# A hybrid decoder layer on one core: logits of b and a with stationary weights, and a last output finished by token halves

## The reference

```python
h = rms_norm(x, norm1_g[l])
proj = h @ w_in[l]                      # two groups of 16 columns are b_logit and a_logit
beta = jax.nn.sigmoid(b_logit)
g = -jnp.exp(a_log) * jax.nn.softplus(a_logit + dt_bias)
...
x = x + jnp.square(jax.nn.relu(h @ w_ff_up[l])) @ w_ff_down[l]
return rms_norm(x, final_norm_g)        # x * rsqrt(mean(x*x) + eps) * gain, per token and channel
```

## Time and profile before

| | |
|---|---|
| median of three runs | 1945.68 us (1942.75, 1945.68, 1945.89) |
| the profiled execution, its own time | 1942.99 us |
| its span, from first to last instruction | 1941.2 us |
| mean granted TensorE clock | 0.989 |
| busy: PE, DVE, ACT, POOL | 97%, 57%, 46%, 6% |
| traffic | 316.36 MB, 163 GB/s |

### The profile page before, as it was taken

How to read it: one execution, slowest core, us unless ns; L and a number is a source line. 1 busy time by engine, 2 the same in 40 slices (tenths; PEclk the granted TensorE clock), 3 DMA queues, 4 the chain that set the end, 5 groups by cost and what they waited for, 6 DMA issues and landing times.

```text
span 1941.2 us, 29129 instructions
## 1 busy us (share of the span) xinstructions
PE 1885.3 (97%) x10816; PEld 1554.7 (80%) x10816; DVE 1099.7 (57%) x1438; ACT 885.4 (46%) x1382; POOL 120.6 (6%) x86
## 2 busy tenths in 40 slices
PE   7998998998998999999999999999999999999997
PEld 6887877877877888888888888888888888888886
DVE  5366676676676665666555555555544455555544
ACT  5344345354354345555444445444433344444442
POOL 0005014014014000000000000000000000000000
PEclk9899999999999999999999999999999999999999
DMA  7353333333333354444456666555555555555553
GB/s 256 126 163 119 110 131 109 110 130 109 115 124 115 114 167 152 141 152 141 161 195 201 201 199 208 183 189 177 191 192 192 192 190 189 185 186 192 195 191 124
DMA packets 87953, 316.36 MB, mean 163 GB/s; under 512 B 9648, under 2 KB 10160, under 8 KB 87728
## 3 DMA queue, kind: packets, MB, share of 16 engines
q1 hardware_dynamic: 86992, 312.64, 48.9%
q0 software_dynamic: 576, 2.10, 0.4%
q10 hardware_dynamic: 288, 0.18, 0.0%
HBM read 312.79 MB, written 2.10 MB: 162 GB/s over the span
## 4 chain that ended last, share of the span: by engine, by line
PE 53%; issue 38%; DVE 3%; POOL 3%; ACT 1%; DMA 0%; DVEq 0%; ACTq 0%; POOLq 0%; SPq 0%
PE acc L287 15%; PE acc L289 14%; PE acc L288 14%; PE J L384 4%; PE J L432 1%; PE J L316 1%; POOL rg L1418 1%; PE J L423 1%; ACT w_hi L653 1%; PE J L440 1%; DVE cT L1051 1%; DVE qn L1051 1%; PE J L475 1%; PE J L304 0%; POOL mats L1440 0%
## 5 line engine op out<-in xcount | busy, mean ns | idle before, releaser
L996 DVE TENSOR_TENSOR w_lo<-raw,w_hi 128x1024 fp32r<-128x1024 f32 x584 | 725.3, 1244 | 638.0 <-ACT w_hi L653 636.6
L653 ACT ACTIVATE w_hi<-raw 128x1024 fp32r<-128x1024 f32 x584 | 618.7, 1061 | 681.7 <-PE acc L289 679.0
L287 PE MATMUL acc<-w_hi,hT_hi 128*128 128x512 f32 x1440 | 582.1, 404 | 8.9 <-issue 4.4
L289 PE MATMUL acc<-w_hi,hT_lo 128*128 128x512 f32 x1440 | 564.7, 392 | 0.0
L288 PE MATMUL acc<-w_lo,hT_hi 128*128 128x512 f32 x1440 | 564.5, 392 | 0.0
L287 PEld LDWEIGHTS acc<-w_hi,hT_hi 128*128 128x128 f32 x1440 | 272.4, 189 | 71.8 <-issue 8.4
L289 PEld LDWEIGHTS acc<-w_hi,hT_lo 128*128 128x128 f32 x1440 | 272.1, 189 | 58.7
L288 PEld LDWEIGHTS acc<-w_lo,hT_hi 128*128 128x128 f32 x1440 | 272.6, 189 | 52.5 <-issue 1.0
L287 PE MATMUL acc<-w_hi,act_hi 128*128 128x512 f32 x512 | 199.3, 389 | 0.0
L289 PE MATMUL acc<-w_hi,act_lo 128*128 128x512 f32 x512 | 199.2, 389 | 0.0
L288 PE MATMUL acc<-w_lo,act_hi 128*128 128x512 f32 x512 | 199.2, 389 | 0.0
(11 more groups left out here) (210 smaller groups left out, 1522.4 us busy)
## 6 DMA issues: line engine op xcount, KB each, us to landing
raw<-weights SPq DMA_DIRECT2D x584, 512.0 KB, 3.3
xres<-x SPq DMA_DIRECT2D x4, 512.0 KB, 7.5
xres<-x POOLq DMA_DIRECT2D x4, 512.0 KB, 5.6
y<-nat SPq DMA_DIRECT2D x4, 512.0 KB, 2.7
fgain_sb<-fgain SPq DMA_DIRECT2D x1, 1024.0 KB, 5.2
masks_sb<-masks SPq DMA_DIRECT2D x1, 640.0 KB, 11.0
zs<-w_ba SPq DMA_DIRECT2D x1, 256.0 KB, 9.9
dist_sb<-dist SPq DMA_DIRECT2D x1, 192.0 KB, 3.4
```

The costliest lines, as they stand in the source:

```text
L287: mm(o, aT_hi[:, kt, tok], w_hi[:, c % RING, w], start=(c == 0 and k == 0), stop=False)
L289: last = mm(o, aT_lo[:, kt, tok], w_hi[:, c % RING, w], start=False, stop=(c == nch - 1 and k == CK - 1))
L653: A(w_hi[:, slot], raw[:, slot], ACT.Copy).then_inc(hi_ready, 1)
L996: tt(w_lo[:, slot], raw[:, slot], w_hi[:, slot].bitcast(F32), ALU.subtract).then_inc(lo_ready, 1)
```

## The change

**Logits.** The weights become the stationary operand (128 x 32) and the activations move, 256 tokens at once: 16 row tiles x 3 matmuls, 48 in all, into `J[0:32, 1, 0:256]`, channels on partitions. DVE copies that to `baT` (in `kn`, not yet in use) at h = 20, PE transposes it in two operations at h = 21 into `J[:, 0]`, where the logits stood before, and DVE's and ACT's decay chain is at h = 22.

**Last output.** Its last four chunks, all four in the ring, are multiplied first for tokens 0 to 127, then for tokens 128 to 255 (`by_halves`). Each half has its own add, square, sums, power, multiplications and four transfers of 256 KB. The channel weight of the first three quarters is multiplied in by POOL while the down projection runs, that of the last quarter by DVE; what is left at the end is a multiplication by the row factor, three of them on DVE and one on ACT for each half. The squares' unused results go to other places. The declarations of semaphores are left out below.

```diff
@@ -174,6 +174,7 @@
         ba = vb[:].rearrange("p t n -> p (t n)")
+        baT = kn[0:32, 0, 0:T]
         kdup = rawg[:, 0]
@@ -255,20 +258,38 @@
             stream(OUT_FF * CPO // RING, N_CHUNKS // RING)
-            for i in range(4):
-                sp.wait_ge(y_ready, i + 1)
-                sp.dma_start(out[:, :, i * NB:(i + 1) * NB], nat[:, :, i * NB:(i + 1) * NB]).then_inc(y_out, 16)
-            sp.wait_ge(y_out, 16 * 4)
+            for t in range(NT):
+                for n, (i, s_done, v) in enumerate(((0, y_dve, 3 * t + 1), (2, y_act, t + 1), (1, y_dve, 3 * t + 2), (3, y_dve, 3 * t + 3))):
+                    sp.wait_ge(s_done, v)
+                    sp.dma_start(out[:, t, i * NB:(i + 1) * NB], nat[:, t, i * NB:(i + 1) * NB]).then_inc(y_out, 16)
+            sp.wait_ge(y_out, 16 * 4 * NT)
...
-            def output(c0, par, aT_hi, aT_lo, free, jobs=None, nch=CPO, h0=0, before=None):
-
-
-                for c in range(nch):
+            def product(par, t, aT_hi, aT_lo, c, k, first, last):
+                kt = c * CK + k
+                w, tok, o = slice(k * NB, (k + 1) * NB), slice(t * P, (t + 1) * P), acc[:, par, t]
+                mm(o, aT_hi[:, kt, tok], w_hi[:, c % RING, w], start=first, stop=False)
+                mm(o, aT_hi[:, kt, tok], w_lo[:, c % RING, w], start=False, stop=False)
+                return mm(o, aT_lo[:, kt, tok], w_hi[:, c % RING, w], start=False, stop=last)
+
+            def by_halves(c0, par, aT_hi, aT_lo, nch):
+
+                for t in range(NT):
+                    for c in range(nch - RING, nch):
+                        if t == 0:
+                            pe.wait_ge(lo_ready, c0 + (c + 1))
+                        for k in range(CK):
+                            ins = product(par, t, aT_hi, aT_lo, c, k, False, c == nch - 1 and k == CK - 1)
+                    ins.then_inc(half_used, 1)
+
+            def output(c0, par, aT_hi, aT_lo, free, jobs=None, nch=CPO, h0=0, before=None, end=None):
+
+
+                for c in range(nch if end is None else end):
                     if before:
@@ -279,15 +300,8 @@
                     for k in range(CK):
-                        kt = c * CK + k
-                        w = slice(k * NB, (k + 1) * NB)
                         for t in range(NT):
-                            tok = slice(t * P, (t + 1) * P)
-                            o = acc[:, par, t]
-                            mm(o, aT_hi[:, kt, tok], w_hi[:, c % RING, w], start=(c == 0 and k == 0), stop=False)
-                            mm(o, aT_hi[:, kt, tok], w_lo[:, c % RING, w], start=False, stop=False)
-                            last = mm(o, aT_lo[:, kt, tok], w_hi[:, c % RING, w], start=False,
-                                      stop=(c == nch - 1 and k == CK - 1))
+                            last = product(par, t, aT_hi, aT_lo, c, k, c == 0 and k == 0, c == nch - 1 and k == CK - 1)
                         if k == CK - 1:
@@ -497,15 +511,19 @@
                     pe.wait_ge(wba_ready, 2)
+                    for kt in range(KT):
+                        w = slice(kt * 32, (kt + 1) * 32)
+                        o = J[0:32, 1, 0:T]
+                        mm(o, wba_hi[:, w], hT_hi[:, kt, :], start=(kt == 0), stop=False)
+                        mm(o, wba_lo[:, w], hT_hi[:, kt, :], start=False, stop=False)
+                        ins = mm(o, wba_hi[:, w], hT_lo[:, kt, :], start=False, stop=(kt == KT - 1))
+                    ins.then_inc(ba_done, 1)
+                if h == 21:
+
+                    pe.wait_ge(baT_ready, 1)
                     for t in range(NT):
-                        tok = slice(t * P, (t + 1) * P)
-                        for kt in range(KT):
-                            w = slice(kt * 32, (kt + 1) * 32)
-                            o = J[:, 0, t * 32:(t + 1) * 32]
-                            mm(o, hT_hi[:, kt, tok], wba_hi[:, w], start=(kt == 0), stop=False)
-                            mm(o, hT_hi[:, kt, tok], wba_lo[:, w], start=False, stop=False)
-                            ins = mm(o, hT_lo[:, kt, tok], wba_hi[:, w], start=False, stop=(kt == KT - 1))
-                    ins.then_inc(ba_done, 1)
+                        ins = tr(J[:, 0, t * 32:(t + 1) * 32], baT[:, t * P:(t + 1) * P], ident[0:32, 0:32])
+                    ins.then_inc(ba_T, 1)
                 if h == 32:
@@ -634,7 +652,9 @@
                            [(relu_sq, r0 + 7 + d)] if d < 2 else [(x_added, x0 + d - 1)],
-                           last_T if d == 0 else None, nch=2 * CPO)
+                           last_T if d == 0 else None, nch=2 * CPO,
+                           end=2 * CPO - RING if hf == 1 and d == FF_DOWN - 1 else None)
+            by_halves(N_CHUNKS - 2 * CPO, 1 - (FF_DOWN - 1) % 2, act_hi, act_lo, 2 * CPO)
@@ -681,7 +701,7 @@
                 for t in range(NT):
-                    ins = A(dst[:, t, w], xres[:, t, w], ACT.Square, accum_out=part[:, t, i:i + 1])
+                    ins = A(dst[:, t], xres[:, t, w], ACT.Square, accum_out=part[:, t, i:i + 1])
                 ins.then_inc(ssq_x, 1)
@@ -838,7 +858,7 @@
                     A(wba_hi[:], w_ba_sb, ACT.Copy).then_inc(wba_ready, 1)
-                if h == 20:
+                if h == 22:
@@ -928,17 +948,17 @@
-            def add_squares(n, first):
+            def add_squares(n, first, dst):
...
                         act.wait_ge(x_added, first + n)
-                        squares(n - 1, nat)
+                        squares(n - 1, dst)
                 return job
...
             for i in range(4):
-                output((OUT_WO + i) * 2, turn_pair(2, i - 1, add_squares(i, 0)) if i else turn_last(1), lambda: None)
+                output((OUT_WO + i) * 2, turn_pair(2, i - 1, add_squares(i, 0, nat[:, :, 0:NB])) if i else turn_last(1), lambda: None)
@@ -965,7 +985,7 @@
                     act.wait_ge(x_added, 4)
-                    squares(3, nat)
+                    squares(3, nat[:, :, 0:NB])
                 for p in range(2):
@@ -976,10 +996,14 @@
                 for n in range(FF_DOWN):
-                    job = up_job(2, 28, r0 + FF_UP) if n == 0 else add_squares(n, 8) if hf == 1 else None
+                    job = up_job(2, 28, r0 + FF_UP) if n == 0 else add_squares(n, 8, rbuf[:, 0]) if hf == 1 else None
                     output(qd + 4 * n, job, lambda: None, nch=2 * CPO)
-            act.wait_ge(x_added, 12)
-            squares(3, nat)
+            for t in range(NT):
+                act.wait_ge(half_added, t + 1)
+                A(rbuf[:, 0, t], xres[:, t, 3 * NB:], ACT.Square, accum_out=part[:, t, 3:4]).then_inc(ssq_x, 1)
+                act.wait_ge(r_x, 5 + t)
+                act.wait_ge(nat_ready, 3)
+                A(nat[:, t, 2 * NB:3 * NB], nat[:, t, 2 * NB:3 * NB], ACT.Copy, scale=row_scale(2, t)).then_inc(y_act, 1)
@@ -1242,6 +1266,9 @@
                     dve.wait_ge(ba_done, 1)
+                    V.tensor_copy(baT, J[0:32, 1, 0:T]).then_inc(baT_ready, 1)
+                if h == 22:
+                    dve.wait_ge(ba_T, 1)
                     for t in range(NT):
@@ -1381,18 +1408,28 @@
                 for n in range(FF_DOWN):
+                    end = hf == 1 and n == FF_DOWN - 1
                     output(qd + 4 * n, up_job(2, 28, r0 + FF_UP) if n == 0 else None,
-                           read(qd + 4 * n + 4, add_x(slice(n * NB, (n + 1) * NB))(1 - n % 2)), nch=2 * CPO)
-
-            row_sums(2)
-            dve.wait_ge(r_x, 5)
+                           (lambda: None) if end else read(qd + 4 * n + 4, add_x(slice(n * NB, (n + 1) * NB))(1 - n % 2)),
+                           nch=2 * CPO)
+
             dve.wait_ge(dist_in, 32)
-            for i in range(4):
-                w = slice(i * NB, (i + 1) * NB)
-                for t in range(NT):
-                    ins = stt(out=nat[:, t, w], in0=xres[:, t, w], scalar=row_scale(2, t), in1=fgain[:, w],
-                              op0=ALU.mult, op1=ALU.mult)
-                ins.then_inc(y_ready, 1)
+            w3 = slice(3 * NB, 4 * NB)
+            for t in range(NT):
+                dve.wait_ge(half_used, t + 1)
+                tt(xres[:, t, w3], xres[:, t, w3], acc[:, 1 - (FF_DOWN - 1) % 2, t], ALU.add).then_inc(half_added, 1)
+                dve.wait_ge(half_added, t + 1)
+                tt(nat[:, t, w3], xres[:, t, w3], fgain[:, w3], ALU.mult).then_inc(nat_link, 1)
+                dve.wait_ge(ssq_x, 16 + t)
+                V.tensor_reduce(stat[:, t:t + 1], part[:, t], AX_X, ALU.add).then_inc(sum_link, 1)
+                dve.wait_ge(sum_link, 3 + t)
+                ts(stat[:, t:t + 1], stat[:, t:t + 1], 1.0 / D, EPS, ALU.mult, ALU.add).then_inc(sum_ready, 1)
+                dve.wait_ge(r_x, 5 + t)
+                dve.wait_ge(nat_ready, 3)
+                dve.wait_ge(nat_link, t + 1)
+                for i in (0, 1, 3):
+                    w = slice(i * NB, (i + 1) * NB)
```

(16 more changed lines are left out.)

## The result

The changed kernel takes 1931.38 us in the median of four runs (1928.9 to 1932.36), the one before 1945.79 (1942.75 to 1948.06): a ratio of 0.9925, 95% interval 0.9908 to 0.9942, 14.4 us less. The profiled execution took 1928.9 us.

What follows compares the result with a forecast made beforehand. PE, busy in 97% of the span, was taken as the bound. Logits 11.5 plus end 5.0 gave 16.5 us, so 1926.5 from 1942.99; 1929.2 if the median's extra 2.7 stays; forecast 1928.0, range 1923.5 to 1932.5.

Steps and rivals of the forecast that it cites:

- The products of the logits: PE's logits: 48 products at 0.113 us each, 5.44 us, replacing 96 that took 15.39 us.
- The transposes: PE at h=21: two transposes of a 32-partition tile, 0.22 us plus 0.03 for the edges.
- rival 1: Logits: the clock falls all the same; 1.8 us less gain, 1929.8, or 1932 with several logit products slowed; chance 0.14.
- the cover of the decay chain: DVE and ACT at h=22: chunk 15 split by 59.8 us, wanted by PE at 62.4, some 2.5 us spare.
- Rival 4: Behind the logits: the decay chain is late, its 2.5 us of cover not sufficing; only shaves the gain; chance 0.03.
- The end: Last output by halves: half the bytes leave earlier, span ends at 1936.2 instead of 1941.2, gain 5.0 us.
- The lower bound: Last output: gain only 4.1 us if halved transfers move at three quarters of the rate, 3.5 us instead of 2.63.
- The estimate from the Trainium skill: Last transfer: fixed 2.0 us plus bytes at 436 GB/s, 2.6 us for 256 KB; gain near 5.4 us.
- Rival 2: Tail gives little: small transfers queue or half 0's chain holds DVE; price 2 to 3 us, 1930.5; chance 0.07.
- One sign: At the end: four output transfers landed while PE still works on half 1.
- POOL's three products: Channel-weight products of 128x1024 moved to POOL: 1.90 us, 4.6 allowed beside DVE, cost 0, some 40 us of cover.
- The sum: Whole kernel: 11.5 us from the logits plus 5.0 us from the end, 16.5 us in all.

Runs made afterwards that it cites:

- logits_128: Changed kernel, each logit product moving 128 tokens instead of 256, 96 products instead of 48; 1929.74 us, one run.
- old_logits_filled: before_fill with one unused 512-column product behind every three old logit products, 32 in all; 1936.1 us, one run.
- premult_only: Kernel before with the new logits and the channel weight multiplied in beforehand, all tokens together, no halves; 1933.76 us.
- halves_only: Changed kernel with its halves, but the channel weight applied at the end, all on DVE, none on ACT or POOL; 1934.23 us.
- two_queues: Changed kernel with two of each half's four output transfers issued from ACT's queue; 1931.58 us, one run.
- tail_only: Changed kernel with the old logits put back, new end kept; 1944.03 us, ratio 0.9981 to the kernel before.
- fill: Changed kernel with ten unused 512-column products ahead of each of PE's two waits per scan group; 1920.23 us, ratio 0.9864 to the kernel before.
- before_fill: Kernel before with ten unused 512-column products ahead of each of PE's two waits per scan group; 1938.39 us, ratio 0.9955.
- inv26: Changed kernel with PE's inversion steps one half chunk later, h = 26 instead of 25; 1921.83 us, ratio 0.9875 to the kernel before.

## Why the prediction was right, and where it was off

The time of 1931.38 us lies in the range, 3.4 us above the forecast; 14.4 us came where 16.5 were summed. Both mechanisms held. That the range holds the time is in part luck: it is 1.1 us below the upper end, and that end stood for a fall of the clock behind the logits, which didn't happen. Point by point:

- **The products of the logits**: 48 x 0.113 = 5.44 us foreseen, 5.46 measured; of the two paces weighed, the one from the rows, 0.113, was nearer to the measured 0.114 than 0.109. That the 0.11 of before was the load, and a narrow load cheaper, is shown by logits_128. **The transposes** were put at 0.25; the two starts of large products around them (51.40 to 51.95 to 52.29, where 0.227 each is the pace) make 0.43.
- **The clock in the logits**: rival 1 did not happen, in any of nine profiles with stationary weights. The reason given, a stream full of columns, fits old_logits_filled and logits_128, one run each. What the sum missed is that the old form's cost is not one number: 17.2 us in the profiled execution, 3.2 more in two others. Hence the logits are worth 11.3 to 14.5 us.
- **The waits**: the cover of the decay chain was 2.5 us by the prediction, 3.9 by the trace. Rival 4 is out.
- **The end**: 5.0 us foreseen, 4.2 measured in every profile. The reading that the transfers bound the end held (premult_only, halves_only, two_queues). The term that was mis-sized is the transfers' own: 1.05 MB move in 3.2 us instead of 2.63, and some 1.15 instead of 0.95 us pass behind the last bytes. The first issue came 0.13 later than foreseen, though a multiplication of 0.48 us instead of 0.43 explains only part of that. The lower bound, 4.1 for three quarters of the rate, was the nearest, in part by luck: the bytes took less than its 3.5 us and the rest more. The estimate from the Trainium skill (DMA: Bandwidth & Descriptors, Anatomy of one DMA) was farther off: it puts a transfer of 256 KB at 2.6 us, and 3.1 were measured. The page gives that figure for the gpsimd path, and these transfers are SP's; and by the prediction's own numbers it makes 1941.2 - 1935.4 = 5.8 us and not 5.4. Rival 2 was true in kind, with 0.8 of its 2 to 3 us. One sign was not met: the first half's transfers had not landed while PE worked on the second half; PE ended at 1918.84, and their bytes flowed until about 1920.4. The prediction's own times said as much (1930.5 against 1928.7), and it cost nothing.
- **POOL's three products**: 3.29 us each, inside the 1.9 to 4.6 allowed, and hidden.
- **The sum**: 11.3 + 4.2 = 15.5, and 14.1 between the two profiled executions. The step that failed is the silent one, that what PE gains early arrives at the end unchanged. In this execution one more half-clock stretch in the first scan group took 1.5 us. Such stretches come and go between executions of the same instructions, each for some 1.5 us. Whether the change makes them likelier stays open. A stretch follows the first wait of the first group in all seven profiles with stationary weights that leave this wait alone, and in tail_only, but not in before; and filling the waits took 11.2 us off the changed kernel's median but 7.7 off that of before.
- **The 2.7 us** between the profiled execution and the median, of which the prediction said that no row told their place: one more stretch in the scan (1.5) and the longer fall in the logits (3.2) have the size for it. Those executions were not profiled, so it isn't shown.

With the scan's scatter out (fill and before_fill, medians of six runs each, not taken side by side), the change is worth 18.2 us. Taken each against the runs of the kernel before beside it, 27.8 and 7.7 us, it is 20.

## What to carry to other kernels

With few output channels make the weights the stationary operand: here a product with 128 loaded and 32 moving columns took 0.112 us, one with 32 loaded and 128 moving 0.060. And the clock stayed at 2.4 GHz over products of 128 or 256 moving columns in all nine profiles, while it fell in all three in which products of 32 moving columns ran alone. Look at the granted clock behind each wait of the bounding engine, here those of 1.8 to 3.0 us: work for nobody placed into such a wait, or a step moved later, can be worth more than the instructions that one was about to save, and it removes most of the scatter that hides small gains. At the end of a kernel ask first whether the last transfers are bound by bytes: then sending a share of them earlier is what helps, here 3.9 of 4.2 us.

## What the runs showed of the hardware that was not expected

PE's wait of 2.7 us in each scan group was followed by 3.4 or 6.8 us at 1.2 GHz in all 32 groups of the eight profiles with the scan unaltered; the wait of 3.0 us ahead of it (1.9 in the fourth group) was so in 18 of 32, in executions of the same instructions; each 3.4 us at 1.2 GHz made the group some 1.5 us longer. A wait of 1.3 us in the same place (inv26) was followed by none in four groups. Waits of 2.0 and 2.5 us elsewhere were followed by such a stretch in before_fill, and one of 2.6 us in the same place was not in before, so no run here gives a limit. Ten unused products in each of the two waits kept 2.4 GHz over the groups in all three kernels that had them. Transfers of 256 KB issued 0.45 us apart moved at 322 to 361 GB/s with a full DMA share, those of 512 KB at 399 with 1.02; why, no run here tells. A one-column power on POOL takes 0.55 us where a two-column one takes 0.70.
